# Banks and second weights of the mixers' output product, and sixteen extra tokens' norm as one batch in the upper product

## The reference

```python
gates = jax.nn.sigmoid(cols(GATE_OFF, N_BRANCH * D_MODEL))
merged = 0
for b, y in enumerate((y_pool, y_fnet, y_hyena, y_na)):
    merged = merged + gates[..., b * D_MODEL:(b + 1) * D_MODEL] * (y @ p['w_branch'][b])
return merged @ p['w_out']                      # token_mixer

x = x + g1 * token_mixer(proj_x, k_c, v_c, p, True)
x = x + g2 * conv_ffn(ada_norm(x, norm2_g[l], sh2, sc2), p)
return rmsnorm(x, final_norm_g)                 # first_block

meta = jnp.broadcast_to(meta_tokens[None].astype(x.dtype), (B, N_META, D_MODEL))
h = jnp.concatenate([meta, x], axis=1)          # second_block
hn = rms_norm(h, attn_norm[i])
```

## Time and profile before

| | |
|---|---|
| three runs | 1760.28, 1760.28, 1762.85 us |
| median | 1760.28 us |
| profiled execution, its own time | 1760.39 us |
| its span | 1758.4 us |
| granted clock of TensorE, mean | 0.974 |
| PE busy | 1674.3 us (95%) |
| PE weight loads busy | 1368.3 us (78%) |
| DVE busy | 915.1 us (52%) |
| ACT busy | 614.1 us (35%) |
| chain that ended last | PE 85%, DVE 9%, ACT 3% |
| moved to or from memory | 170.28 MB, mean 97 GB/s |

### The profile page before, as it was taken

How to read it: one execution, slowest core, us unless ns; L and a number is a source line. 1 busy time by engine, 2 the same in 40 slices (tenths; PEclk the granted TensorE clock), 3 DMA queues, 4 the chain that set the end, 5 groups by cost and what they waited for, 6 DMA issues and landing times.

```text
span 1758.4 us, 20355 instructions
## 1 busy us (share of the span) xinstructions
PE 1674.3 (95%) x8091; PEld 1368.3 (78%) x8091; DVE 915.1 (52%) x1269; ACT 614.1 (35%) x791; POOL 96.4 (5%) x134
## 2 busy tenths in 40 slices
PE   8899988999998899999989999998998999999997
PEld 3478867788886778888878889977876878888886
DVE  4755576576665554444344564244665554444333
ACT  2342348322222333333333433234553332222221
POOL 0100000110110000000000100003431000000000
PEclk9999979999999899999999999998999999999998
DMA  9321101644653133332323421231111333332331
GB/s 324 111 93 61 48 25 49 193 154 133 215 166 116 53 97 96 96 96 83 97 72 109 124 73 51 73 100 53 38 31 49 96 91 101 96 96 67 99 99 48
DMA packets 213924, 170.28 MB, mean 97 GB/s; under 512 B 5444, under 2 KB 202948, under 8 KB 213830
## 3 DMA queue, kind: packets, MB, share of 16 engines
q1 hardware_dynamic: 207222, 144.80, 27.7%
q0 software_dynamic: 6608, 24.19, 4.1%
HBM read 166.84 MB, written 2.13 MB: 96 GB/s over the span
## 4 chain that ended last, share of the span: by engine, by line
PE 85%; DVE 9%; ACT 3%; issue 1%; DMA 0%; DVEq 0%; SPq 0%; ACTq 0%
PE PS L434 23%; PE PS L436 23%; PE PS L435 23%; PE PS L2080 2%; DVE WL L92 1%; PE PS L558 1%; DVE T L92 1%; PE PS L452 1%; PE PS L453 1%; PE PS L454 1%; PE PS L2065 1%; ACT WH L88 1%; PE PS L2057 1%; PE PS L2058 1%; PE PS L2059 1%
## 5 line engine op out<-in xcount | busy, mean ns | idle before, releaser
L434 PE MATMUL PS<-XH,WH 128*128 128x512 f32 (+1 forms) x1280 | 487.4, 381 | 8.0 <-DVE WL L92 7.0
L435 PE MATMUL PS<-XL,WH 128*128 128x512 f32 (+1 forms) x1280 | 484.0, 378 | 0.0
L436 PE MATMUL PS<-XH,WL 128*128 128x512 f32 (+1 forms) x1280 | 483.7, 378 | 0.0
L92 DVE TENSOR_TENSOR WL<-WS,WH 128x2048 fp32r<-128x2048 f32 (+1 forms) x129 | 272.4, 2112 | 246.8 <-ACT WH L88 245.4
L434 PEld LDWEIGHTS PS<-XH,WH 128*128 128x128 f32 x1280 | 239.8, 187 | 55.5 <-DVE WL L92 8.0
L436 PEld LDWEIGHTS PS<-XH,WL 128*128 128x128 f32 x1280 | 239.6, 187 | 45.7
L435 PEld LDWEIGHTS PS<-XL,WH 128*128 128x128 f32 x1280 | 239.7, 187 | 44.1
L88 ACT ACTIVATE WH<-WS 128x2048 fp32r<-128x2048 f32 (+1 forms) x129 | 228.6, 1772 | 72.9 <-PE PS L436 48.6
L434 PE MATMUL PS<-HH,WH 128*128 128x512 f32 x352 | 138.2, 393 | 4.8 <-DVE WL L92 4.8
L435 PE MATMUL PS<-HL,WH 128*128 128x512 f32 x352 | 137.8, 391 | 0.0
L436 PE MATMUL PS<-HH,WL 128*128 128x512 f32 x352 | 137.7, 391 | 0.0
(11 more groups left out here) (358 smaller groups left out, 2391.1 us busy)
## 6 DMA issues: line engine op xcount, KB each, us to landing
WS<-in_w_in SPq DMA_DIRECT2D x24, 1024.0 KB, 5.2
WS<-in_ffn_w_up SPq DMA_DIRECT2D x44, 512.0 KB, 5.1
WS<-in_ffn_w_in SPq DMA_DIRECT2D x44, 512.0 KB, 5.0
MSRC<-in_w_mod POOLq DMA_DIRECT2D x32, 512.0 KB, 4.8
WS<-in_fox_w_in SPq DMA_DIRECT2D x16, 1024.0 KB, 5.6
WS<-in_ffn_w_down SPq DMA_DIRECT2D x16, 704.0 KB, 4.7
WS<-in_ffn_w_out SPq DMA_DIRECT2D x16, 704.0 KB, 4.8
MODW<-in_w_mod SPq DMA_DIRECT2D x8, 1024.0 KB, 11.0
```

The lines of the kernel that those rows point to most:

```text
L92: self.e.tensor_tensor(o, a, b, op).then_inc(*self.done.to(*key))
L434: e.matmul(o, lh, rh, start=first and i == 0, stop=False)
L435: e.matmul(o, lh, rl, start=False, stop=False)
L436: ins = e.matmul(o, ll, rh, start=False, stop=last and i == n - 1)
```

## The change

out1's eight tiles get the banks 1, 7, 2, 0, 1, 2, 0, 1; PE waits ahead of i = 0 for branch 57 instead of 62, and for branch 58 and 63 ahead of tiles 2 and 3. ACT's copy of chunk OUT1 + 1 moves from the start of out1 to between the MGH of k = 6 and of k = 7, DVE's subtraction to right behind MGL of k = 7. The spread of the sixteen tokens' factor and the copy of it move from i = 0 to i = 1. The sixteen tokens' norm leaves down1; in its place DVE makes two products over all eight slices at once behind HL of f = 8 in up1, ACT one copy, and DVE one subtraction behind HL of f = 9.

```diff
@@ gate_act
                 split_act(a, MGH[:, k, :], T[m][:, :], ("mg_hi", k))
+                if k == 6:
+                    hi_chunk(a, OUT1 + 1)
@@ out1_bank, out1_pe
-        return bank((6, 7)[n] if n < 2 else n % 3)
+        return bank((1, 7, 2, 0, 1, 2, 0, 1)[n])
...
-                e.wait_ge(*dve.at("branch", 62))
+                e.wait_ge(*dve.at("branch", 57))
...
-                    if n >= 5:
-                        e.wait_ge(*dve.at("out1", n - 3))
+                    if n < 4:
+                        e.wait_ge(*dve.at("branch", 56 + n if n == 2 else 63))
+                    else:
+                        e.wait_ge(*dve.at("out1", n - 3 if n > 4 else 1))
...
-            if i == 0:
+            if i == 1:
                 spread_pe(e, "meta", 16)
-            if i == 1:
                 e.wait_ge(*dve.at("out1", 1))
@@ out1_act
-            hi_chunk(a, OUT1 + i + 1)
+            if i:
+                hi_chunk(a, OUT1 + i + 1)
@@ out1_dve
+        lo_chunk(v, OUT1 + 1)
         g2 = VOFF["norm2_g"]
...
-            lo_chunk(v, OUT1 + i + 1)
+            if i:
+                lo_chunk(v, OUT1 + i + 1)
...
-            if i == 0:
+            if i == 1:
                 e.wait_ge(*pe.at("meta", "spread"))
                 v.cp(MRMS, bank(3, 16), key=("meta_rms",))
-            if i == 1:
                 modv_add_dve(v, 23)
@@ up_act, behind HH
+            if conv and f == META_AT:
+                meta_act(a)
@@ up_dve, behind HL
+            if conv and f == META_AT:
+                meta_scale_dve(v)
+            if conv and f == META_AT + 1:
+                meta_rest_dve(v)
@@ down1_act, down1_dve
-            if k == 1:
-                meta_act(a)
...
-            if k == 1:
-                meta_dve(v)
@@ META_AT = 8
     def meta_act(a):
-        for k in range(8):
-            normed_act(a, "metan", k, SQ[:, k, 0:16], XH[:, k, 0:16])
...
+        a.e.wait_ge(*dve.at("metan", "scaled"))
+        a.act(XH[:, :, 0:16], SQ[:, :, 0:16], ACT.Copy, key=("metan", "hi"))
+
+    def meta_scale_dve(v):
+        g = VOFF["attn_g"]
+        v.tt(SQ[:, :, 0:16], META[:, :, :], MRMS.unsqueeze(1).broadcast_to([128, 8, 16]), ALU.mult)
+        v.tt(SQ[:, :, 0:16], SQ[:, :, 0:16], VT[:, g:g + 8].unsqueeze(2).broadcast_to([128, 8, 16]), ALU.mult,
+             key=("metan", "scaled"))
+
+    def meta_rest_dve(v):
+        v.e.wait_ge(*acts.at("metan", "hi"))
+        v.tt(XL[:, :, 0:16], SQ[:, :, 0:16], XH[:, :, 0:16].bitcast(F32), ALU.subtract, key=("metan", "lo"))
```

More of the change, by code:

```diff
@@ L1614, in down1_dve @@
                 v.tt(RST[:, 0:L], RST[:, 0:L], T[1][:, :], ALU.add, key=("norm3", "sum", k))
-            if k == 1:
-                meta_dve(v)
+    META_AT = 8
     def meta_act(a):
-        for k in range(8):
-            normed_act(a, "metan", k, SQ[:, k, 0:16], XH[:, k, 0:16])
-    def meta_dve(v):
-        normed_dve(v, "metan", lambda k: META[:, k, :], 16, vecs("attn_g"), None, sq_cell(0, 16), xh_cell(0, 16),
-                   xl_cell(0, 16), MRMS)
+        a.e.wait_ge(*dve.at("metan", "scaled"))
[8 more added lines that the diff above has]
+        v.tt(XL[:, :, 0:16], SQ[:, :, 0:16], XH[:, :, 0:16].bitcast(F32), ALU.subtract, key=("metan", "lo"))
     def full_norm_dve(v, name, gain, before):
@@ L1755, in foxp_pe @@
                 if m == 0:
-                    e.wait_ge(*dve.at("metan", "lo", 7))
+                    e.wait_ge(*dve.at("metan", "lo"))
                 if m == 1:
```

## The result

| | before | after |
|---|---|---|
| median of the first comparison (4 runs each) | 1761.57 us | 1744.23 us |
| lowest to highest | 1760.28 to 1765.76 | 1743.31 to 1745.85 |
| ratio | | 0.9892, 95% interval 0.9873 to 0.9911 |
| profiled execution | 1760.39 us, span 1758.4 | 1745.85 us, span 1743.8 |
| ratio of a second comparison on another chip (r1_changed_again, 4 runs against 7) | | 0.9903, 0.9886 to 0.9919 |

The forecast was 1745.3 us, with a range of 1742.3 to 1749.3. The changed kernel came in at 1744.23, 1.1 us under the forecast. The forecast was counted down from 1760.28, the median known then; in this comparison the kernel before had 1761.57. By the medians the gain is thus 17.34 us, 2.35 more than the 14.99 foreseen, and 1.29 of these are hidden in the time by the higher start.

The account below looks back on a forecast made before the run. PE, busy 1674.3 of 1758.4 us, was taken as the bound, with only its waits and slow-clock stretches to win. Gains of 7.85 (out1) and 7.14 us (down1), 14.99 together, gave 1745.3 us, range 1742.3 to 1749.3.

Parts of the forecast that it names:

- Both waits named: PE's waits at out1's start (6.05 us, for branch 62) and in down1 (4.66 us, for WL).
- Part 1: Out1's first chunk: new banks end the 6.05 us wait; row 7 starts at 550.46; with Part 2 gains 7.85 us.
- Part 2: Out1's i = 1: WL split ahead cuts a 2.3 us wait to about 1.0; with Part 1 gains 7.85 us.
- the row at 617.90: Profile row: a product lasting 0.50 us after a 1.21 us wait, taken to show the 1.0 us wait costs no clock.
- the sum: Whole kernel: 7.85 us from out1 plus 7.14 us from down1, 14.99 us gained.
- Part 3: Down1: without the norm, the next X addition comes 7.14 us earlier, 4.66 of wait and 2.48 of slow products.
- Part 4: Up1, f = 8: the norm batch delays WH by 1.63 us, rounded to 1.7, under 2.07 us of cover; cost 0.
- Rival 1: Later slow stretches, after the changed places, grow or shrink by about 2.6 us: 1747.9 or 1742.7 us; chance 0.08.
- section on a rule: Slow stretches at 1205 to 1211 and behind 1333.61 are drawn anew, as slow products behind the same wait vary.
- Rival 2: A new wait gets slow products: ahead of out1's i = 1, 1748.2 us, or up1's batch, 1746.1; chance 0.06.
- rival 3: Out1 stays bound by a misread bank or late split; only down1's 7.14 us remain, 1753.1 us; chance 0.04.
- rival 4: Late weights for OUT1+1 hold up ACT's mg_hi 7 and out1; slower than before, e.g. 1764.2 us; chance 0.02.

Follow-up runs that it names:

- r1_changed_again: The changed kernel unaltered, run again beside e10 on another chip; 0.9903 of the kernel before, median 1745.07 us.
- e2: The changed kernel with out1 put back as before (banks, order of WH and WL, spread), the norm batch kept in up1; 0.9953 of the kernel before.
- e1: The changed kernel with the sixteen tokens' norm put back slice by slice into down1, out1's changes kept; 0.9945 of the kernel before.
- e3: The changed kernel without the early split of chunk OUT1+1; last gate product to out1's second chunk 13.72 us, against 12.42 in the changed kernel.
- e7: The kernel before with 26 unread products ahead of PE's wait for branch 62; last gate product to out1's second chunk 17.82 us, against 20.52.
- e6: The changed kernel with the norm slice by slice, in up1 at f = 8; out1's second chunk to down1's first X addition 304.23 us, against 301.18.
- e4: The changed kernel with out1's banks and waits of before, early split kept; last gate product to out1's second chunk 20.29 us, against 12.42.
- e8: The changed kernel with WH products ahead of WL ones in first tiles of gates, out1, up1, up2, down1, down2; 0.9869 of the kernel before.
- e10: e8 with the same product order also in the projection and the attention's gate; 0.9874 of the kernel before, median 1740.40 us.
- e5: The changed kernel with the norm batch in down1's k = 1 instead of up1; X additions k = 1 to 2 16.83 us apart, against 14.96.

## Why the prediction was right, point by point

**What bounds the kernel.** Both waits named were the ones that went: 6.05 and 4.66 us are in no list of the changed kernel. e2 brings back the first alone, e1 the second.

**Part 1.** Foreseen: row 7 of the first chunk waits for the last MGL and starts 10.01 us behind the last gate product (550.46 - 540.45). Measured: 552.26 - 542.23 = 10.03. PE is hidden behind DVE's branches there, as put.

**Part 2.** Foreseen: i = 1 at 12.34 us behind the last gate product; measured D1 12.42. DVE left 0.11 us ahead of WL and not 0.04. The wait was put at 1.0 us and is 0.72 in the trace, but with the modelled end of the product before it: from start to start the delay is 554.65 - 553.54 - 0.23 = 0.88. It cost no clock, as the row at 617.90 had said, and e3 shows the same up to 2.04 us. The X addition came at 555.72, 13.49 behind the last gate product, against 13.35 foreseen. Part 2's 2.3 us without the split ahead is e3's 2.04.

D1 falls by 8.10 and not by the 7.85 of the sum, but 0.33 of that only moved: the sum was counted from the start of the spread at 560.64, D1 from the product behind it at 560.97. On the sum's footing the gain is 7.77. The spread was said to cost in its new place what it cost in the old, and so it does. It now stands ahead of the small sums (565.76, and 566.08 for the sums), and the product behind both starts 1.10 us behind the one ahead of them; in the kernel before, with the sums alone, that distance is 0.59. The next part, which takes in these 0.51 us, still did not grow (301.20, 301.18), and this is luck. Eight small sums ahead of up1, for which PE waits 2.32 us in both kernels, ran at another clock, before and after:

```profile
596.70 1.59 PE L462 MATMUL PS<-ONE,T 128*128 128x1 f32 x8 [2.32 <-DVE T L92]
590.90 1.02 PE L462 MATMUL PS<-ONE,T 128*128 128x1 f32 x8 [2.32 <-DVE T L92]
```

The granted clock was 0.60 in 596.6 to 598.4 before and 1.00 in 590.8 to 592.0 after. The forecast has no such term. The sums took 1.02 us in all seven profiles that have both the new banks and the split ahead, and 1.39 to 1.84 us in the other five; why is open.

**Part 3.** 7.14 us foreseen and 7.14 measured between the profiles. That the term is exact is luck in one half of it: the 4.66 us are fixed, but the number of slow products was read from the one profile with which the result is then compared; e1 and e7 show that for the same wait the term may be 6.4 or 6.6.

**Part 4.** The chain was put at 1.63 to 1.7 us, measured 1.71 (WH starts 2.46 us behind the start of HH instead of 0.75). The elements' times, 0.29 and 0.31 us, came out of the interpolation between the rows of 16 and of 512 or 2048 elements as they are; broadcast operands cost nothing extra. The cover was read too large. It was taken up to the modelled end of a product (716.12), which overlaps the next, whereas PE's first product of the next chunk starts at 715.97 in the kernel before. So the cover was 1.92 us and not 2.07, and 0.20 were left instead of 0.37, of which PE needs the 0.05 from a DVE end to its start. e6 bears out 1.92 from the other side: its WH starts 5.57 us behind the start of HH instead of 0.75, so 4.82 later, and PE would start 4.82 - 1.92 + 0.05 = 2.95 us late. It starts at 710.64 instead of 707.70, 2.94 late. The cost of 0 in the sum stood, with half the margin that was foreseen.

**The rivals.** Rival 1 (the slow stretches elsewhere change) happened, on both sides at once and small in sum: 1.78 us lost ahead of the change, 1.15 won behind it. The loss begins near 47 us, in fourteen products on which both kernels are the same, before and after:

```profile
47.52 6.55 PE L593 MATMUL PS<-FWC,FS 65*128 65x512 f32 x14
46.65 10.21 PE L593 MATMUL PS<-FWC,FS 65*128 65x512 f32 x14
```

The granted clock fell from 1.00 to 0.50 there in the changed kernel, although PE had been busy without a pause since 30.9; before, it stayed at 1.00. By the first product of the projection (68.74 before, 73.75 after) the changed kernel is 5.01 us late. A shorter wait for DVE further on (4.00 us instead of 6.42) and faster sums behind it take up most of that, so that 1.78 are left.

The gain behind the change is the case that the forecast's section on a rule had in mind. By the Trainium skill's page "TensorE: Matmul & The Clock Gate", Part 1, the number of slow products behind the same wait varies. The traces agree, with ten slow products behind the 4.66 us in the kernel before and six in e1. So they do for nearly the same wait ahead of the attention's output product, here in the changed kernel (4.24 us, and 4.31 in the earlier trace rows):

```profile
1319.52 2.08 PE L2118 MATMUL PS<-SUMS,E 128*128 128x512 f32 x2 [4.24 <-DVE SUMS L111]
...
1321.82 0.63 PE L453 MATMUL PS<-KO,WH 128*128 128x512 f32 x1
1322.24 0.55 PE L454 MATMUL PS<-QO,WL 128*128 128x512 f32 x1
1322.62 0.39 PE L452 MATMUL PS<-QO,WH 128*128 128x512 f32 x1
```

The products are fast 3.1 us behind the end of that wait. In the kernel before, they were so only 4.3 us behind it (timeline of PE), and about 0.5 of the 1.15 us come from there:

```profile
1337.18 0.62 PE L453 MATMUL PS<-KO,WH 128*128 128x512 f32 x1
1337.61 0.42 PE L454 MATMUL PS<-QO,WL 128*128 128x512 f32 x1
1337.88 0.40 PE L452 MATMUL PS<-QO,WH 128*128 128x512 f32 x1
```

Rival 2 is refuted by the clock of 1.00 and by e3; rival 3 by D1; rival 4 by ACT's 4.07 us idle ahead of the last MGH.

**What is still open.** The two comparisons give 17.3 and 17.6 us by the medians (19.0 and 17.1 by the ratios), the landmarks 15.3. That the time itself was hit within 1.1 us is in part luck, since the kernel before was 1.3 us slower in the comparison than in the runs from which the forecast was counted. The forecast's 15.0 us are inside the interval of the second comparison and just outside that of the first (0.9915 against 0.9911). Part of it can be that slow products now come at two places fewer; but what they cost in the profile before, 2.87 and 2.48 us, was no low value (e4 has 2.97 at the first place, e7 and e1 have 1.90 and 1.73 at the second). The runs don't tell whether the rest is scatter.

## What to carry to other kernels

When one engine waits for a buffer, look which of the readers in front is the last, and take the buffers in the order in which they come free: here a list of eight bank numbers, with the waits that go with it, gave 6.8 us. Then work out at once what is late next and from how much cover, because the second wait (here 2.0 us, cut to 0.7) is already in the trace. Small steps that two engines pass to and fro should be one batch, and put where the cover is longer than their whole chain, counted up to the instruction that is queued behind it; in e6 a moved step of 4.4 us, under 1.9 us of cover, lost 3.05 of the 7.14 us. Read the cover from start to start of the products, not from a modelled end.

## What the runs showed that was not expected

- The kernel before scattered more than the first three runs showed: 1760.16 to 1769.05 us in 19 runs on one chip, against 1760.28 to 1762.85. The time to the last gate product was between 539.50 and 545.22 us in the ten profiles of kernels that are the same up to there (all but e8 and e10). It falls into two groups: in the six where the fourteen products of L593 took 6.55 us it is 539.50 to 540.45, in the four where they took 10.06 to 10.45 (the changed kernel, e1, e2, e5) it is 542.20 to 545.22.
- Between products of 512 columns PE's clock did not fall for waits of 1.57, 2.04 and 2.79 us (e5, e3, e6), and did for 4.66 and 6.05 us. At 4.66 us the loss behind the wait was 2.48, 1.90 and 1.73 us in three profiles. A wait is not all: the clock also fell at L593 while PE was busy, and behind the 2.32 us ahead of the small sums in the kernel before.
- Doing the products that don't need the late operand first took 6.0 of the 7.1 us of waits on WL away, and no landmark of e8 shows a cost of the other order of products.
